# Row numbers from the one-hot table made by GpSimd instead of VectorE, with spread vectors and convolution taps in other places, in a hybrid decoder step

## The chip, the cores and the metric

The kernel runs on one core of a Trainium2 chip. The metric is the device time of one execution in microseconds, smaller is better; times are medians of several runs. The core has TensorE (PE, with its weight loads as PEld), VectorE (DVE), ScalarE (ACT), GpSimd (POOL) and the queue engine SyncE (SP). All inputs start in HBM, and 16 DMA engines carry them to the on-chip memory.

## What is computed

A two-layer decoder trunk on 256 prompt tokens and 32 sample tokens (8 sequences of 4), width 1024, all in float32. Each layer has a mixing part and an expert part:

```python
h  = rmsnorm(x) @ w_in                       # columns split among the mixers and gates
yA = gelu(u) * (tril(W_s) @ layernorm(gelu(v)) + b)          # chunks of 128, 8 groups
yB = silu(layernorm(causal_depthwise(val * sigmoid(gate))))  # 31 taps
yM = attention(q, memory)                                     # 4 heads, 256 tokens
x += (sig(gA)*(yA@w_oA) + sig(gB)*(yB@w_oB) + sig(gM)*(yM@w_oM)) @ w_out

xn = rmsnorm(x);  q = xn @ wq                # 8 heads, two halves of 64
v1, i1 = top_k(q1 @ keys1, 16);  v2, i2 = top_k(q2 @ keys2, 16)
cand   = v1[:, None] + v2[None, :];  cv, ci = top_k(cand.reshape(256), 16)
eid    = i1[ci // 16] * 128 + i2[ci % 16]    # expert row numbers, of 16384
hid    = gelu(xn . u_tab[eid]);  x += sum(softmax(cv) * hid * v_tab[eid])
```

## The kernel before

**Portions, steps and pairs.** Tokens are worked in four portions: portions 0 and 1 are the two halves of layer 0 (128 prompt tokens; 128 prompt and 32 sample tokens), 2 and 3 those of layer 1. A portion first has its mixing, which ends with scores against the keys, and then 8 or 10 expert steps. A step serves 16 tokens with 8 heads, that is 128 partitions with 16 experts each, in 8 pairs (k = 0 to 7) of two experts per partition. There are 36 steps (s) and 288 pairs (t).

**A pair.** GpSimd issues two indirect gathers (L610), each of 128 rows of 8 KB, u and v side by side. They go to one of 5 slots, so pair t + 5 is asked for when TensorE has done pair t (semaphore `v_used`). VectorE makes the two dot products of u with the token's row (`dots`, L1660; the trace shows each as a custom instruction with a short read of the sum). ScalarE makes gelu and a diagonal of weights (L663, L1024), and TensorE adds the weighted v rows (L2441).

**The order of work.** Each engine walks over the pairs. Between pairs a `stepper` advances that engine's program of the next portion's mixing as far as `reach` allows, by a table of places (`parts`, PLACE). So portion m + 1's mixing runs beside portion m's experts, in an order that is fixed for every engine. Only portion 0's mixing has no experts beside it (the first 290 us).

**Picking experts.** For step s + 1, VectorE does `pick_pairs` after the dots of pair k = 0 of step s: the sums of candidates, the top 16 of 256, and the semaphore `cmax`. After the dots of k = 1 it does `pick_experts` (L1619 to L1639). The candidate's number is split in two, a one-hot table of 32 x 16 is made, multiplied by the key numbers and summed, and 128 times the one number plus the other is written to `ids`, with the semaphore `ids`, for which the first gather of step s + 1 waits. `scale_fold` (L1672) makes the gate-weighted fold matrices, `shift` gives `cmax`. The two halves' top 16 of step s + 2 (`pick_half`) follow k = 6 and 7.

**Taps.** The causal convolution of a portion's prompt tokens is 62 taps: `conv(n)` does the next n of them. A tap is four VectorE instructions of 128 x 128 (L1131; L1129 for the first tap of a half). `beside(name, n)` and `gated(first, last, taps)` place them between the other steps of the mixing. Semaphore `conv` tells TensorE that all are done, for the sums over channels (`csum`).

**SP's queue.** SP issues the weight pieces of 1 MB in a ring of 4 (L474), each when TensorE has done with the piece four before. Some go to places of their own (`kept`, `kept_half`). In between it issues stores and other loads, each with its own wait: convolution states are stored behind the last `glu` of a portion (L532 to L534). The spread vectors (L550, L552) are four small vectors of layer 0, each repeated to 128 partitions by DMA, into parts of the expert buffers that portion 0's mixing does not use otherwise.

Of the kernel before, what the change touches and what calls it, by code (L numbers as in the profile page):

```python
# [12 lines left out]
P = 128  # L13
# [26 lines left out]
PAIRS = 8  # L40
# [200 lines left out]
def build(nc, x_in, consts_in, mem_in, cache_in, state_in, w_in, small_in, vecs_in, fing_in, ws_in, wss_in,  # L241
          keys_in, uv_in, y_out, memk_out, memv_out, convp_out, convs_out, vn_out):
    with ExitStack() as ctx:
# [193 lines left out]
        def _(sp):  # L437
# [63 lines left out]
            for m in range(PORTIONS):  # L501
# [9 lines left out]
                for n, it in enumerate(items(m)):  # L511
# [34 lines left out]
                    if m == 0 and (kind, i) == ("mg", 12):  # L546
                        sp.dma_start(x[:, 1], x_in[:, 1]).then_inc(x_landed[1], 16)
                    if m == 0 and (kind, i) == ("va", 2):
                        for to, rows in ((ln_rows[0], LN_G), (ln_rows[1], LN_B), (bs_rows, BS)):
                            sp.dma_start(to, vecs_in[rows, :].rearrange("k c -> (k c)").unsqueeze(0).to_broadcast([P, D])).then_inc(  # L550
                                spread_landed, 16)
                        sp.dma_start(ffn_row, vecs_in[FFN_G, :].rearrange("k c -> (k c)").unsqueeze(0).to_broadcast([P, D])).then_inc(row_landed, 16)  # L552
# [31 lines left out]
        def _(pool):  # L584
            def gather(t):
# [22 lines left out]
                for i in range(2):  # L608
# [4 lines left out]
                    ).then_inc(uv_landed[b], 16)  # L613

            def mixing(m):
                l, p = m // 2, m % 2
# [34 lines left out]
            for m in range(PORTIONS):  # L651
                mix = first if m == 0 else stepper(mixing(m + 1)) if m + 1 < PORTIONS else None
                for u in range(PAIRS * STEPS[m % 2]):
                    t = PAIRS * FIRST[m] + u
                    if t + SLOTS < PAIRS * NSTEP:
                        gather(t + SLOTS)
                    if mix:
                        mix(reach(m + 1, u - 1))
# [430 lines left out]
        def _(dve):  # L1089
# [29 lines left out]
            def mixing(m):  # L1119
# [164 lines left out]
                else:  # L1284
# [4 lines left out]
                    V.tensor_tensor(ys, ys, conv_b.unsqueeze(2).to_broadcast([P, KB, T_S]), ALU.add).then_inc(S["conv_s"], 1)  # L1289
                    yield from beside("q0", 1)  # L1290
                    yield from att_max(0)
                    yield from beside("q1", 2)
                    yield from att_max(1)
                    yield from beside("q2", 1)
                    att_norm(0)
# [11 lines left out]
                    if m in CACHED:  # L1307
# [8 lines left out]
                        max_sample(1)  # L1316
                    yield place["va3"]
                for t in range(1 + p):
                    r = ROWS[t]
# [146 lines left out]
                else:  # L1466
                    taps = 1 if m in CACHED else 3
                    yield from gated(0, 3, taps)
# [4 lines left out]
                    yield from spatial()  # L1473
                    yield from gated(8, 12, 3)
                    conv(2 * CONV_W)
# [51 lines left out]
            def pick_half(s, half):  # L1527

                if half == 0:
                    m = next(i for i in range(PORTIONS) if s < FIRST[i + 1])  # L1530
                    dve.wait_ge(S["score"], at("score", m, s - FIRST[m] + 1 if m else s))
# [22 lines left out]
            def pick_pairs(s):  # L1554

                sum_pairs()
                top16(cand_v, cand_i, cand, rest)
                dve.drain()
                shift(s)
# [23 lines left out]
            def pick_first():  # L1583
# [32 lines left out]
                shift(0)  # L1616

            def pick_experts(s, l):
                V.tensor_scalar(ab_u[:, 0:16], cand_i, 4, None, ALU.logical_shift_right)  # L1619
                V.tensor_scalar(ab_u[:, 16:32], cand_i, 15, None, ALU.bitwise_and)  # L1620
                dve.drain()
                V.tensor_copy(ab_f, ab_u)
                dve.drain()
                oh3 = onehot.rearrange("p (k a) -> p k a", a=16)
                V.tensor_tensor(oh3, ab_f.unsqueeze(2).to_broadcast([P, 32, 16]),  # L1625
                                iota16.unsqueeze(1).to_broadcast([P, 32, 16]), ALU.is_equal)
                dve.drain()
                for half in range(2):
                    part = oh3[:, 16 * half:16 * half + 16]
                    V.tensor_tensor(part, part, top_if[:, 16 * half:16 * half + 16].unsqueeze(1).to_broadcast([P, 16, 16]), ALU.mult)  # L1630
                dve.drain()
                V.tensor_reduce(pick_k, oh3, AX.X, ALU.add)
                dve.drain()
                V.scalar_tensor_tensor(out=eid_f, in0=pick_k[:, 0:16], scalar=float(NK), in1=pick_k[:, 16:32], op0=ALU.mult, op1=ALU.add)
                dve.drain()
                if s == NSTEP - 1:
                    for half in range(2):
                        V.tensor_scalar(ids_last[:, 2 * half:2 * half + 2], eid_f[:, 14:16], 2.0, float(2 * NEXP * l + half), ALU.mult, ALU.add)
                V.tensor_scalar(ids[:, 16 * (s % 2):16 * (s % 2) + 16], eid_f, float(NEXP * l), None, ALU.add).then_inc(S["ids"], 1)  # L1639

# [81 lines left out]

            def layer(s):
                return next(i for i in range(PORTIONS) if s < FIRST[i + 1]) // 2

            V.memset(one, 1.0).then_inc(one_set, 1)
# [9 lines left out]
            for m in range(PORTIONS):  # L1736
                mix = first if m == 0 else stepper(mixing(m + 1)) if m + 1 < PORTIONS else None
                for u in range(PAIRS * STEPS[m % 2]):
# [6 lines left out]
                    if k == 0 and s + 1 < NSTEP:  # L1745
                        pick_pairs(s + 1)
                    elif k == 1 and s + 1 < NSTEP:
                        pick_experts(s + 1, layer(s + 1))
                    elif k == 3 and s + 1 < NSTEP:
# [811 lines left out]
```

## Time and profile before

| | |
|---|---|
| median of 3 runs | 2242.09 us (2241.83 to 2243.29) |
| the profiled execution | 2242.79 us, span 2241.0 us |
| PE, DVE, ACT, POOL busy | 73%, 71%, 29%, 30% of the span |
| DMA | 895.56 MB, mean 400 GB/s |
| of it by gathers (software queue) | 604.02 MB |

A busy share is an average over stages with different limits. The profile's row of DMA over 40 slices of the span reads 9 (90% or more) in most slices, so it has to be read with the GB/s beside it, which lie at 421 or so in the full slices. DMA shares can read a little over 1. An idle time in brackets behind a row is that engine's idle time just before it, and the name is who ended it.

### The profile page before, as it was taken

How to read it: one execution, taken by the hardware profiler on the slowest of the kernel's cores; microseconds unless marked ns; L12 is line 12 of the kernel's file. 1: busy time of each engine (PE TensorE's matmuls, PEld its weight loads, DVE VectorE, ACT ScalarE, POOL GpSimd, SP SyncE). 2: the span in 40 equal slices, each digit the busy share in tenths (PEclk: the TensorE clock that was granted, in tenths of full speed). 3: DMA queues.
4: the chain of work that ended last, by engine and by line, in shares of the span. 5: the costliest groups of instructions: out<-in, count | busy, mean ns of one | idle time of the engine just before them, and what ended most of it. 6: DMA issues, size and time to landing. Idle time of an engine off the chain costs nothing.

```text
span 2241.0 us, 31369 instructions
## 1 busy us (share of the span) xinstructions
PE 1631.8 (73%) x10944; PEld 1068.0 (48%) x10944; DVE 1582.7 (71%) x4234; ACT 656.3 (29%) x1647; POOL 674.7 (30%) x596
## 2 busy tenths in 40 slices
PE   9999986889797477878788547776999854334334
PEld 8855675667585144644434315643877620000002
DVE  4454289898766667877776568977876686776775
ACT  3121243411423241423123223342223323322222
POOL 0000032232232432332223243221323354454443
PEclk9999998899897588899889777876999875555556
DMA  8699899999999999999999999999999999999998
GB/s 298 245 379 413 322 408 421 402 404 358 366 402 419 421 421 421 421 421 421 421 377 422 421 421 421 421 403 405 404 419 421 411 393 421 422 421 421 422 421 334
DMA packets 127772, 895.56 MB, mean 400 GB/s; under 512 B 16096, under 2 KB 16928, under 8 KB 20480
## 3 DMA queue, kind: packets, MB, share of 16 engines
q0 software_dynamic: 83232, 604.02, 65.4%
q1 hardware_dynamic: 44384, 289.54, 32.1%
q8 instruction: 88, 1.44, 0.3%
q14 instruction: 68, 0.56, 0.1%
HBM read 885.39 MB, written 8.11 MB: 399 GB/s over the span
## 4 chain that ended last, share of the span: by engine, by line
DMA 32%; PE 31%; DVE 21%; issue 8%; ACT 4%; DVEq 3%; POOL 2%; SPq 0%; POOLq 0%; ACTq 0%
DMA uv<-uv_in,idx_u 23%; PE bank L1785 14%; DVE uv L1660 10%; DMA ring<-w_in 7%; PE bank L2441 5%; PE bank L1791 4%; PE bank L2097 3%; DVE yB L1131 3%; DMA ring<-cache_in 2%; POOL uv L610 1%; ACT L663 1%; DVE x L1683 1%; DVEq L1126 1%; ACT diag L1024 1%; DVE pick L1625 1%
## 5 line engine op out<-in xcount | busy, mean ns | idle before, releaser
L610 POOL DMA_INDIRECT uv<-uv_in,idx_u x574 | 658.5, 1147 | 1345.5 <-PE bank L2441 642.9
L1660 DVE CUSTOM_DVE_ANT_0 uv<-uv,xrep 128x1024 f32<-128x1024 f32 x576 | 682.2, 1223 | 210.5 <-DMA uv<-uv_in,idx_u 204.7
L2441 PE MATMUL bank<-uv,diag 128*32 128x512 f32 x2176 | 393.5, 804 | 461.5 <-ACT diag L1024 457.2
L1785 PEld LDWEIGHTS bank<-xnT,ring 128*128 128x128 f32 x3168 | 433.9, 201 | 77.9 <-issue 66.4
L1785 PE MATMUL bank<-xnT,ring 128*128 128x160 f32 (+1 forms) x3168 | 456.0, 304 | 2.1 <-DMA ring<-w_in 2.0
L663 ACT ACTIVATE pick<-pick 128x2 f32<-128x2 f32 (+1 forms) x315 | 66.9, 212 | 1054.1 <-DVE pick L1660 1051.1
L2441 PEld LDWEIGHTS bank<-uv,diag 128*32 128x32 f32 x2176 | 49.8, 122 | 649.7 <-ACT diag L1024 590.7
L1131 DVE SCALAR_TENSOR_TENSOR yB<-ext_p,small,yB 128x128 f32<-128x128 f32 x960 | 275.6, 349 | 19.6
L663 ACT ACT_TABLE_LOAD x137 | 175.8, 1283 | 2.4
L1024 ACT ACTIVATE diag<-gated_fold,pick 128x32 f32<-128x32 f32 x574 | 153.1, 314 | 9.8 <-ACT pick L663 0.3
L2097 PE MATMUL bank<-ring,xnT 128*128 128x512 f32 x192 | 86.7, 605 | 0.0
L1785 PE MATMUL bank<-yMA,ring 128*128 128x160 f32 x512 | 76.9, 306 | 5.0 <-ACT yMA L663 5.0
L1785 PEld LDWEIGHTS bank<-yMA,ring 128*128 128x128 f32 x512 | 73.7, 196 | 5.2 <-ACT yMA L663 5.2
L663 ACT ACTIVATE phase<-bank 128x512 f32<-128x512 f32 (+2 forms) x44 | 23.3, 529 | 168.1 <-PE bank L1785 67.1
L1008 ACT ACTIVATE xrep<-xnf 32x1024 f32<-32x1024 f32 x64 | 67.4, 1053 | 1.4
L1791 PE MATMUL bank<-ring,ext_s 128*128 128x256 f32 x256 | 60.6, 397 | 0.0
L663 ACT ACTIVATE yMA<-bank 128x256 f32<-128x256 f32 (+2 forms) x54 | 22.2, 410 | 129.2 <-PE bank L1785 71.7
L2097 PE MATMUL bank<-ring,yMA 128*128 128x512 f32 x128 | 58.0, 605 | 1.2 <-DMA ring<-w_in 1.2
L2434 PE MATMUL bank<-uv,diag 128*32 128x256 f32 x256 | 28.6, 588 | 41.4 <-ACT diag L1024 40.8
L2097 PEld LDWEIGHTS bank<-ring,xnT 128*128 128x128 f32 x192 | 36.2, 193 | 46.1 <-issue 44.8
L663 ACT ACTIVATE sg<-bank 128x160 f32<-128x160 f32 (+1 forms) x80 | 23.6, 295 | 117.1 <-PE bank L1785 116.9
L1785 PE MATMUL bank<-ext_s,ring 128*128 128x256 f32 x256 | 57.1, 381 | 0.0
(323 smaller groups left out, 1844.4 us busy)
## 6 DMA issues: line engine op xcount, KB each, us to landing
ring<-w_in SPq DMA_DIRECT2D x211, 1024.0 KB
uv<-cache_in SPq DMA_DIRECT2D x16, 1024.0 KB, 9.7
ring<-cache_in SPq DMA_DIRECT2D x16, 1024.0 KB
uv<-uv_in,idx_u POOLq DMA_INDIRECT x578, 13.9
uv<-w_in SPq DMA_DIRECT2D x4, 1024.0 KB, 10.0
ring<-w_in SPq DMA_DIRECT2D x6, 512.0 KB, 4.9
ext_s<-state_in SPq DMA_DIRECT2D x2, 1088.0 KB, 16.7
convs_out<-ext_s SPq DMA_DIRECT2D x2, 1088.0 KB
```

Of the source, the lines that this page charges most:

```text
L610: nc.gpsimd.indirect_dma_start(out=uvbuf[2 * b + i], out_offset=None, in_=uv_in, in_offset=bass.IndirectOffsetOnAxis(ap=ids[:, c:c + 1], a ...
L663: ins = nc.scalar.activation(out, in_, func, bias=bias, scale=scale, **({} if accum is None else {"accum_out": accum}))
L1008: ins = nc.scalar.activation(xrep[gg % 2][32 * i:32 * (i + 1), :], xnf[1 if t == 2 else 0][r0:r0 + 32], ACT.Copy)
L1024: ins = nc.scalar.activation(diag[:, t % 4, i], gated_fold[:, c], ACT.Copy, scale=gel[:, 16 * (s % 2) + c:16 * (s % 2) + c + 1])
L1126: dve.drain()
L1131: ins = V.scalar_tensor_tensor(out=yB[:, c, 0:P], in0=ext_p[:, c, w:w + P], scalar=wconv[:, c, w:w + 1], in1=yB[:, c, 0:P], op0=ALU.mult, ...
L1660: ins = V.tensor_tensor_reduce(out=u, in0=u, in1=xrep[gg % 2][:, :], scale=1.0, scalar=0.0, op0=ALU.mult, op1=ALU.add, accum_out=hid[:, c: ...
L1785: ins = MM(out, w[:, k, P * b:P * (b + 1)], rhs(k), start=k == 0, stop=k == KB - 1)
L1791: ins = MM(out, lhs(k), w[k], start=k == 0, stop=k == KB - 1)
L2097: ins = MM(out[:, :], rows[:, 4 * (i % 2) + k, 0:P], w[:, k, :], start=i % 2 == 0 and k == 0, stop=i % 2 == 1 and k == 3)
L2434: ins = MM(vbank[gg % 2][32 * q:32 * (q + 1), 0:256], diag[:, t % 4, i], uvbuf[2 * b + i][:, c:c + 256], start=first and i == 0, stop=last ...
L2441: ins = MM(vbank[gg % 2][c:c + 32, :], diag[:, t % 4, i], uvbuf[2 * b + i][:, D + 512 * n:D + 512 * (n + 1)], start=first, stop=last)
```

## The change

The change has three parts. The row numbers are made by GpSimd: VectorE makes the one-hot table at the end of `pick_pairs`, before it gives `cmax`; GpSimd waits for `cmax` behind the gathers of the pair that k = 0 frees, and does the multiplication, a sum in four halving steps, the two steps of the number and the copy to `ids`. VectorE waits for `ids` before it writes the shared buffer again. The spread vectors are issued behind the load of mk 1 instead of va 2. And 16 taps of portion 1 stand elsewhere: one more at q0 and at q2 and two more at va3, one less at each of the columns 0 to 7, one more at each of the columns 8 to 11.

```diff
-                    if m == 0 and (kind, i) == ("va", 2):
+                    if m == 0 and (kind, i) == ("mk", 1):
                         for to, rows in ((ln_rows[0], LN_G), (ln_rows[1], LN_B), (bs_rows, BS)):
...
+            def pick_experts(s):
+
+                l = next(i for i in range(PORTIONS) if s < FIRST[i + 1]) // 2
+                pool.wait_ge(S["cmax"], s + 1)
+                oh3 = onehot.rearrange("p (k a) -> p k a", a=16)
+                oh4 = onehot.rearrange("p (h k a) -> p h k a", h=2, a=16)
+                G = nc.gpsimd
+                G.tensor_tensor(oh4, oh4, top_if.rearrange("p (h a) -> p h a", h=2).unsqueeze(2).to_broadcast([P, 2, 16, 16]), ALU.mult)
+                for n in (8, 4, 2):
+                    G.drain()
+                    G.tensor_tensor(oh3[:, :, 0:n], oh3[:, :, 0:n], oh3[:, :, n:2 * n], ALU.add)
+                G.drain()
+                G.tensor_tensor(pick_k.unsqueeze(2), oh3[:, :, 0:1], oh3[:, :, 1:2], ALU.add)
+                G.drain()
+                G.tensor_scalar(eid_f, pick_k[:, 0:16], float(NK), float(NEXP * l), ALU.mult, ALU.add)
+                G.drain()
+                G.tensor_tensor(eid_f, eid_f, pick_k[:, 16:32], ALU.add)
+                G.drain()
...
+                G.tensor_copy(ids[:, 16 * (s % 2):16 * (s % 2) + 16], eid_f).then_inc(S["ids"], 1)
...
                     if t + SLOTS < PAIRS * NSTEP:
                         gather(t + SLOTS)
+                    if t % PAIRS == 0 and t // PAIRS + 1 < NSTEP:
+                        pick_experts(t // PAIRS + 1)
                     if mix:
                         mix(reach(m + 1, u - 1))
...
-                    yield from beside("q0", 1)
+                    yield from beside("q0", 1 if m in CACHED else 2)
...
-                    yield from beside("q2", 1)
+                    yield from beside("q2", 1 if m in CACHED else 2)
...
                     yield place["va3"]
+                    if m == 1:
+                        conv(2)
...
-                    taps = 1 if m in CACHED else 3
+                    taps = 1 if m in CACHED else 2
...
-                    yield from gated(8, 12, 3)
+                    yield from gated(8, 12, 3 if m in CACHED else 4)
...
                 if half == 0:
+                    dve.wait_ge(S["ids"], s)
...
                 sum_pairs()
                 top16(cand_v, cand_i, cand, rest)
+                dve.drain()
+                V.tensor_scalar(ab_u[:, 0:16], cand_i, 4, None, ALU.logical_shift_right)
+                V.tensor_scalar(ab_u[:, 16:32], cand_i, 15, None, ALU.bitwise_and)
+                dve.drain()
+                V.tensor_copy(ab_f, ab_u)
+                dve.drain()
+                V.tensor_tensor(onehot.rearrange("p (k a) -> p k a", a=16), ab_f.unsqueeze(2).to_broadcast([P, 32, 16]),
+                                iota16.unsqueeze(1).to_broadcast([P, 32, 16]), ALU.is_equal)
                 dve.drain()
                 shift(s)
...
-            def pick_experts(s, l):
...
-                    elif k == 1 and s + 1 < NSTEP:
-                        pick_experts(s + 1, layer(s + 1))
```

SP's queue in portion 0, before, from the cached pieces ahead of va 2 on (names are destination and source; `uv<-vecs_in` are the spread vectors):

```order
L483 DMA uv<-cache_in 128x2048 x2
L467 DMA ring<-w_in 128x1024
L472 DMA kept_half<-w_in 128x1024
L550 DMA uv<-vecs_in 128x1024 x3
L552 DMA uv<-vecs_in 128x1024
L454 DMA kept<-w_in 128x2048
L540 DMA memv_out<-phase 128x2048
```

And in the changed kernel, where they stand now:

```order
L516 DMA ext_s<-mem_in 128x2048
L518 DMA x<-x_in 32x1024
L474 DMA ring<-w_in 128x2048 x7
L550 DMA uv<-vecs_in 128x1024 x3
L552 DMA uv<-vecs_in 128x1024
L474 DMA ring<-w_in 128x2048 x5
L483 DMA uv<-cache_in 128x2048 x2
```

The four transfers went from in front of `kept` to between the seventh and the eighth of those twelve ring pieces.

VectorE in the third step of portion 0, before, from the end of the dots of k = 1 to portion 1's normalisation statistics (BN_STATS):

```order
L1660 ISA pick 128x1
L1619 TENSOR_SCALAR idx_u<-idx_u 128x16
L1620 TENSOR_SCALAR idx_u<-idx_u 128x16
L1622 CAST pick<-idx_u 128x32
L1625 TENSOR_TENSOR pick<-pick,consts 128x512
L1630 TENSOR_TENSOR pick<-pick 128x256 x2
L1632 TENSOR_REDUCE pick<-pick 128x32
L1634 SCALAR_TENSOR_TENSOR pick<-pick 128x16
L1639 TENSOR_SCALAR idx_u<-pick 128x16
L1672 TENSOR_TENSOR gated_fold<-consts,pick 128x256
L1322 BN_STATS stat<-phase 128x6 x2
```

The same place in the changed kernel, from the end of `pick_pairs` on (L1593 makes the table, L1674 is the dots, L1157 the taps, L1350 the statistics):

```order
L1593 TENSOR_TENSOR pick<-pick,consts 128x512
L1581 TENSOR_SCALAR pick<-pick,stat 128x1
L1674 ISA uv,pick<-uv,xrep 128x1024
L1674 ISA pick 128x1
L1674 ISA uv,pick<-uv,xrep 128x1024
L1674 ISA pick 128x1
L1157 SCALAR_TENSOR_TENSOR yB<-ext_p,small,yB 128x128 x8
L1350 BN_STATS stat<-phase 128x6 x2
```

The table is made ahead of the dots of k = 1, the rest has left VectorE, two taps stand in front of the statistics, and the fold's scaling has gone behind them.

GpSimd, before, around portion 1's mixing:

```order
L640 AFFINE_SELECT phase<-phase 128x1024
L628 COPY ext_p<-ext_p 128x8x30
L610 DMA uv<-uv_in,idx_u 128x2048 x58
L640 AFFINE_SELECT phase<-phase 128x1024
L643 AFFINE_SELECT phase<-phase 32x256
```

And in the changed kernel, for the first of its 35 steps with row numbers:

```order
L610 DMA uv<-uv_in,idx_u 128x2048 x12
L622 TENSOR_TENSOR pick<-pick 128x512
L625 TENSOR_TENSOR pick<-pick 128x32x8
L625 TENSOR_TENSOR pick<-pick 128x32x4
L625 TENSOR_TENSOR pick<-pick 128x32x2
L627 TENSOR_TENSOR pick<-pick 128x32
L629 TENSOR_SCALAR pick<-pick 128x16
L631 TENSOR_TENSOR pick<-pick 128x16
L637 CAST idx_u<-pick 128x16
L610 DMA uv<-uv_in,idx_u 128x2048 x16
```

Eight operations stand between the gathers of pair 5 and those of pair 6, and so in every step: between the gathers that k = 0 and k = 1 free.

## Rows read from the trace of the kernel before

**Rows 1.** Busy time by engine, clock, DMA share, GB/s, in portion 0's mixing.

```profile
core 0: us, PE busy (x) PEld busy (x) DVE busy (x) ACT busy (x) POOL busy (x), PEclk, DMA share, GB/s
40.00:50.00 10.00, 9.98 (x58) 9.11 (x59) 7.43 (x26) 1.45 (x4) 0.00 (x0) 1.00 0.44 147
140.00:150.00 10.00, 6.72 (x36) 4.83 (x34) 3.41 (x13) 1.21 (x4) 0.00 (x0) 0.83 0.99 415
160.00:220.00 60.00, 60.00 (x328) 34.94 (x329) 26.60 (x73) 5.58 (x11) 1.48 (x2) 1.00 1.01 420
```

**Rows 2.** The same view of later stretches.

```profile
480.00:520.00 40.00, 29.73 (x183) 25.18 (x185) 37.66 (x108) 7.26 (x20) 9.71 (x10) 0.87 0.96 373
560.00:600.00 40.00, 27.27 (x179) 22.37 (x177) 31.11 (x72) 12.12 (x25) 9.01 (x9) 0.87 0.89 344
650.00:1120.00 470.00, 349.42 (x2251) 223.20 (x2249) 341.31 (x920) 140.25 (x361) 153.49 (x140) 0.83 1.01 421
1120.00:1200.00 80.00, 69.05 (x226) 30.24 (x227) 59.70 (x153) 29.49 (x60) 19.74 (x18) 0.89 0.99 391
1800.00:1810.00 10.00, 5.69 (x91) 2.00 (x89) 9.18 (x27) 3.02 (x13) 5.54 (x5) 0.99 0.88 328
1840.00:2160.00 320.00, 121.87 (x504) 12.73 (x504) 239.68 (x589) 94.63 (x247) 153.73 (x127) 0.50 1.01 421
```

**Rows 3.** TensorE in order of time: start, us, line, operation, [idle before <-releaser].

```profile
131.12 3.72 PE L1791 MATMUL bank<-ring,xnT 128*128 128x256 f32 x16
...
143.88 5.41 PE L1791 MATMUL bank<-kept,xnT 128*128 128x256 f32 x16 [3.28 <-DMA kept<-w_in]
...
159.98 7.35 PE L2097 MATMUL bank<-ring,yMA 128*128 128x512 f32 x16 [1.16 <-DMA ring<-w_in]
```

**Rows 4.** SP's queue in order of time.

```profile
127.26 1.47 SPq L550 DMA_DIRECT2D uv<-vecs_in  x3
...
129.29 0.45 SPq L454 DMA_DIRECT2D kept<-w_in  x1
```

**Rows 5.** VectorE in order of time, the third step's pick.

```profile
426.59 0.17 DVE L1619 TENSOR_SCALAR idx_u<-idx_u 128x16 uint32<-128x16 uint32 x1
...
427.94 0.76 DVE L1630 TENSOR_TENSOR pick<-pick 128x256 f32<-128x256 f32 x2
...
429.88 0.42 DVE L1672 TENSOR_TENSOR gated_fold<-consts,pick 128x256 f32<-128x256 f32 x1
```

**Rows 6.** VectorE and TensorE in order of time, portion 1's mixing.

```profile
439.04 1.43 PE L1785 MATMUL bank<-yMA,ring 128*128 128x160 f32 x4 [5.00 <-ACT yMA L663]
...
461.87 3.57 DVE L1131 SCALAR_TENSOR_TENSOR yB<-ext_p,small,yB 128x128 f32<-128x128 f32 x12
...
548.66 0.32 DVE L1352 SCALAR_TENSOR_TENSOR sg<-sg,bank 128x160 f32<-128x160 f32 x1 [0.81 <-ACT sg L663]
...
573.30 4.57 PE L2166 MATMUL bank<-yB,consts 128*128 128x160 f32 x16 [5.11 <-DVE yB L1131]
```

**Rows 7.** GpSimd and VectorE side by side at 482 us; GpSimd's copy by line.

```profile
480.40 3.92 DVE L1131 SCALAR_TENSOR_TENSOR yB<-ext_p,small,yB 128x128 f32<-128x128 f32 x8
482.09 1.11 POOL L640 TENSOR_SCALAR_AFFINE_SELECT phase<-phase 128x1024 f32<-128x1024 f32 x1
483.14 0.52 POOL L643 TENSOR_SCALAR_AFFINE_SELECT phase<-phase 32x256 f32<-32x256 f32 x1
...
L637 POOL COPY uv<-yMA 128x256 f32<-128x256 f32 x1 | 0.4, 399 | 93.6 <-ACT yMA L663 93.6
```

**Rows 8.** The tail: gathers of a pair on GpSimd, and that pair's dots.

```profile
1886.23 1.97 POOL L610 DMA_INDIRECT uv<-uv_in,idx_u  x1 [2.69 <-DVE idx_u L1639]
1888.50 0.94 POOL L610 DMA_INDIRECT uv<-uv_in,idx_u  x1 [0.31 <-issue]
...
1904.74 1.23 DVE L1660 CUSTOM_DVE_ANT_0 uv<-uv,xrep 128x1024 f32<-128x1024 f32 x1 [2.25 <-DMA uv<-uv_in,idx_u]
```

**Rows 9.** The chain of waits at 363 us; VectorE in order of time.

```profile
363.56 31.05 DMA ring<-w_in
...
406.38 0.42 DVE L1226 TENSOR_REDUCE stat<-bank 128x1 f32<-128x256 f32 x1 [7.13 <-PE bank L1917]
```

More of the change, by code:

```diff
@@ L613, in gather @@
                     ).then_inc(uv_landed[b], 16)
+            def pick_experts(s):
[15 more added lines that the diff above has]
+                G.drain()
+                if s == NSTEP - 1:
+                    for half in range(2):
+                        G.tensor_scalar(ids_last[:, 2 * half:2 * half + 2], eid_f[:, 14:16], 2.0, float(half), ALU.mult, ALU.add)
+                    G.drain()
+                G.tensor_copy(ids[:, 16 * (s % 2):16 * (s % 2) + 16], eid_f).then_inc(S["ids"], 1)
             def mixing(m):
@@ L1616, in pick_first @@
                 shift(0)
-            def pick_experts(s, l):
[L1619 to L1639, printed above, removed]
             def gates(s):
@@ L1721, in last_norm @@
                 V.scalar_tensor_tensor(out=y_last, in0=x_last, scalar=rstd_last, in1=fing_last, op0=ALU.mult, op1=ALU.mult).then_inc(y_rows, 1)
-            def layer(s):
-                return next(i for i in range(PORTIONS) if s < FIRST[i + 1]) // 2
             V.memset(one, 1.0).then_inc(one_set, 1)
```

## The prediction

> **What bounds the kernel now.** I read the stretches first [rows 1, 2]. DMA is the floor: from 650 to 1120 us it moves 421 GB/s at a busy share of 1.01, and again from 1840 to 2160 us, where the expert rows alone are fetched. In such a stretch nothing that VectorE saves or loses is seen, as long as gathers keep coming. Time can be won or lost only where DMA falls short. There are four such places. In the first 290 us no gather runs, and TensorE is full but for a hole at 140 us, where DMA is full, while it was 0.44 busy at 40 to 50 us [rows 1]. From 400 to 640 us, where portion 1's mixing runs beside portion 0's experts, DMA falls to 344 GB/s at its lowest. Two short ones follow, at 1120 to 1200 and at 1800 to 1810 us [rows 2]. Then I read who waits for whom in each.
>
> The hole at 140 us is TensorE waiting 3.28 us for the kept weights and 1.16 us for ring weights; 16 matmuls that take 3.72 us at the full clock took 5.41 us behind the hole [rows 3]. The kept weights are issued on SP's queue right behind the four spread vectors [rows 4]. From 406 to 640 us the chain of waits changes hands. VectorE begins at 406.38 behind TensorE, and from then to 434 us has no wait of note; TensorE stands 5.00 us for what follows from it at 439.04 [rows 5, 6]. From 439 to 456 TensorE leads. From 456 to 508 VectorE is full (37.66 of 40 us at 480 to 520 [rows 2]); from 508 to 548 TensorE leads; from 548 to 573.30 VectorE does, and TensorE stands 5.11 us for the convolution [rows 6]. After that TensorE and ScalarE lead to 650 us.
>
> **Part 1, the spread vectors: -5.0 us.** They are 4 transfers of 0.5 MB. At 421 GB/s that is 5.0 us of DMA taken out of the full stretch ahead of the kept weights, and 2 us of issuing [rows 4]. At their new place, behind the load of mk 1, which waits for the seventh of eight glu pieces, they run ahead of 60 us, where DMA is under half busy; q 1 stands behind them and is needed two weight pieces later. That is the cover; without it they would cost up to their 5.0 us again. What TensorE can win is 3.28 + 1.16 us of waits and 5.41 - 3.72 = 1.7 us of slow matmuls, 6.1 us; but the ring weights at 159.98 come through a DMA that stays full, and can be only 5.0 us earlier. So 5.0, at least 2 (issue time alone).
>
> **Part 2, the row numbers: what VectorE gives up.** In a step (the third, as all of them), the four instructions from L1619 to L1625 take 426.59 to 427.94 us, 1.3 us, and move to the pair before. The rest, L1630 to L1639, ends at 429.88: 1.9 us, which leaves VectorE [rows 5]. Cost if nothing else happened: -1.9 us for each step that VectorE leads.
>
> **What GpSimd takes back.** The trace has no two-input operation on GpSimd, so I bound it. A copy of 256 elements took 0.40 us, a select of 1024 1.11 us [rows 7]: 0.16 us plus 0.93 ns an element. The eight new operations are 512, 256, 128, 64, 32 and three times 16 elements. The three large ones are 1.3 us at this rate and 2.1 us if a second input doubles it; the five small ones 0.2 us each. And such an operation holds VectorE up. While GpSimd did its two selects at 482 us (1.11 and 0.52 us), eight taps that take 2.4 us elsewhere took 3.92 [rows 6, 7], 1.5 us more: the first select cost about its own length, the short one a third of it. I take 2.1 + 5 x 0.07 = 2.4 us lost per step where VectorE has two-input work all the time, the two-read end for the large ones, since these are two-input, and the short select for the small ones. Ends: 0 if a multiply or add of GpSimd does not exclude VectorE as the select did, 3.1 us if the small ones block at full length. So a step that VectorE leads changes by -1.9 + 2.4 = +0.5 us, not by -1.9. The Trainium skill (SBUF - State Buffer, "SBUF: two separate sides") says that GpSimd and a VectorE instruction with two SBUF inputs take an exclusive lock for a whole instruction, which speaks against this change; [rows 7] agree for the long select. It also prices a GpSimd two-input add of 2048 elements at 4.5 us (GPSIMD Engine Reference, "Elementwise - side-by-side cycle accounting"); by that the large three would be an estimated 2.0 us and the step about the same. No row here shows such an add.
>
> The steps that count: three in portion 1's mixing (the third, fourth and fifth), one at 1120 and one at 1805 us. In the third, GpSimd begins behind its gathers, and part of its work falls on the normalisation statistics, which read one input; 1.9 us there, so 0. The last two give +0.5 each. The other 30 lie under a full DMA.
>
> GpSimd's gathers stand behind the new work. In the tail the pair whose dots run at 1904.74 is issued from 1886.23 to 1889.4 [rows 8]. Less 5.0 us for its own 2 MB and 3 us that I allow for latency, it could be issued 7 us later without being missed. The row numbers would begin some 2 us ahead of 1886.23, behind the gathers of the pair before, so they may last some 9 us; I expect 3 to 5. Cost 0. SP does not stand behind GpSimd.
>
> **The moved 1.3 us before the stores.** SP waits for the last glu block of portion 1, then issues the stores and, from 363.56 us, loads; the piece of va that TensorE stands for lands 31 us later [rows 9]. In that step the 1.3 us now lie ahead of the glu block: +1.3 us (0 if the full DMA evens it out).
>
> **Part 3, the taps.** 12 instructions take 3.57 us with the end of the last [rows 6], so a tap (four) is 1.21 us. Two more (q0, q2) fall before 406 us, where VectorE has 7.13 us to spare [rows 9]: 0. Two more ahead of the statistics are on the path to 439.04: +2.4. Of the eight taken from columns 0 to 7, three lie where TensorE leads: 0; five lie between 456 and 508: -6.05. Four more in columns 8 to 11 give +4.84, less 0.81 us that VectorE waited at 548.66 [rows 6]: +4.0. There the scaling of the fold (0.42 us) now stands behind the taps: -0.4. Taps in all: 2.4 - 6.05 + 4.0 - 0.4 = -0.05 us.
>
> **Sum.** -5.0 (spread), +1.3 (glu block), steps 0 + 0.5 + 0.5 in portion 1, -0.05 (taps), +0.5 + 0.5 later: -1.75 us. The profiled execution took 2242.8 us (span 2241.0), so 2241.0; the median of the runs shown is 0.7 us under it: 2240.4.
>
> **Rivals.**
> VectorE isn't blocked. For it: only one place in the trace shows the blocking at length, and GpSimd may run where VectorE waits or does one-input work (max, find index). Against it: behind the pick come dots and taps, all two-input. Five steps then give -1.9 instead of up to +0.5: 0.0 - 4 x 2.4 - 1.9 = -11.5 us against the forecast, 2229; blocked by half, 2234.6. Chance 0.27.
> The spread vectors give little: at 160 to 220 us DMA is at 420 GB/s [rows 1] and could be the limit just behind TensorE. Then -2 in place of -5: 2243.4. Chance 0.11.
> TensorE takes up portion 1's additions, since VectorE's and TensorE's leads alternate and each hides some of the other's: +4.0 at 548 us halves, 2238 or a little under. Chance 0.06.
> Slower: the row numbers come too late. If each of the eight operations waits for a dot product of 1.22 us in turn, they take 3 + 8 x 1.22 = 12.8 us. From 9 us on, each further us empties the DMA queue once per step; over some 26 steps under a full DMA, 12.8 us would be +99 us, and 10 us already +26. For it: gathers already stretch from 0.94 to 1.97 us beside dots [rows 8]. Against it: in the tail VectorE has 10 us of 40 free [rows 2]. A milder form, the upper bound of blocking in all five steps and the third step too (+0.7 each, +1.2 there) with the stores' delay doubled, is 2246. Chance of over 0.2% slower: 0.14.
> The forecast itself: 0.42, its own range 2236 to 2245.
>
> **How the numbers follow.** About 0.2%, 4.5 us, can be told from no change, so faster means below 2237.6. That is the first rival (0.27), the third where it falls there (0.04) and the low end of the forecast (0.07): 0.38. Slower: 0.14 and the high edge of the second, 0.16. Same: 0.46. The range reaches down to most of the first rival, 2230, and up to the mild slow case, 2247.
>
> **What the profile after would show.** No wait for the kept weights near 140 us, and the first gather 5 us earlier. GpSimd's eight operations, some 3 us in sum, and taps or dots beside them of 1.9 us in place of 1.22. From the first dots to the convolution's end at 573 us about the same distance (+1 to +5 us from 456 being lost and won again), DMA at 420 again from 650 us. I am wrong if the dots beside GpSimd's operations keep 1.22 us, if the stretch from 400 to 640 us shrinks by 5 us or more, or if DMA falls under 415 GB/s in the tail.

## The result: 220 us slower

| kernel | median | runs | to the kernel before, 95% interval |
|---|---|---|---|
| before | 2242.69 us | 4 (2241.83 to 2247.23) | |
| changed | 2462.47 us | 4 (2461.13 to 2463.80) | 1.0977 (1.0963 to 1.0991) |

The forecast was 2240.4 us, its range 2230 to 2247. One of the four executions of a kernel further down, the one with sixteen fills, took 4397 us beside three of 2313 to 2325 us, and its median and ratio are those of the three. The page of the changed kernel, its span, VectorE's and DMA's rows over 40 slices, and the chain of waits:

```profile
span 2462.1 us, 31650 instructions
PE 1651.1 (67%) x10944; PEld 1077.4 (44%) x10944; DVE 1581.7 (64%) x4057; ACT 656.2 (27%) x1647; POOL 796.2 (32%) x878
...
DMA  8799999998988899899999889899998888788878
GB/s 311 281 395 364 371 367 408 376 380 345 392 364 352 352 386 379 361 410 377 383 405 381 344 341 396 329 420 399 379 408 337 354 354 350 295 358 350 352 293 350
DMA packets 127775, 895.58 MB, mean 364 GB/s; under 512 B 16096, under 2 KB 16928, under 8 KB 20480
...
issue 27%; PE 25%; DMA 22%; DVE 11%; POOL 6%; POOLq 5%; ACT 2%; DVEq 2%; SPq 0%
```

The bytes are the same, the rate has gone from 400 to 364 GB/s, and of the slices that read 421 before none is left (the best reads 420). VectorE is as busy as before (1582.7 us then). "issue" with 27% is time in which an engine stood for nothing that the profile names. The stretches, in the columns of [rows 1]:

```profile
650.00:1120.00 470.00, 317.44 (x2033) 202.28 (x2032) 301.60 (x767) 133.22 (x340) 175.64 (x193) 0.80 0.91 373
1840.00:2160.00 320.00, 143.51 (x1078) 61.69 (x1077) 191.77 (x453) 83.90 (x226) 133.09 (x144) 0.62 0.83 341
```

Against [rows 2], 421 GB/s became 373 beside mixing (the first stretch) and 341 in the tail (the second): the floor itself has holes. What the change brought to GpSimd's queue comes once per step, so I looked there. GpSimd and VectorE in order of time, in one step of the tail (L610 the gathers, L622 the multiplication, L625 the three larger additions, L637 the copy to `ids`, L1674 the dots):

```profile
2225.94 1.07 POOL L610 DMA_INDIRECT uv<-uv_in,idx_u  x1 [0.30 <-issue]
2227.02 1.45 POOL L622 TENSOR_TENSOR pick<-pick 128x512 f32<-128x512 f32 x1
...
2244.03 1.23 DVE L1674 CUSTOM_DVE_ANT_0 uv<-uv,xrep 128x1024 f32<-128x1024 f32 x1 [3.50 <-DMA uv<-uv_in,idx_u]
2244.55 3.11 POOL L625 TENSOR_TENSOR pick<-pick 128x256 f32<-128x256 f32 x3 [16.08 <-issue]
2245.18 1.73 DVE L1674 CUSTOM_DVE_ANT_0 uv<-uv,xrep 128x1024 f32<-128x1024 f32 x1
...
2248.90 0.20 POOL L637 CAST idx_u<-pick 128x16 uint32<-128x16 f32 x1
2249.65 0.99 POOL L610 DMA_INDIRECT uv<-uv_in,idx_u  x1 [0.55 <-POOL idx_u L637]
```

The multiplication starts at once behind the gathers, and then GpSimd stands for 16.08 us. Between the two lies only the first `G.drain()` (L624). It ends at 2244.5, half a us after the dots of the last pair issued (2244.03) found their rows landed. That half a us comes back: in 20 of the 35 steps VectorE stood waiting for that same pair, and in every one of the 20 the drain ended 0.51 or 0.52 us after these dots began. In the other 15 VectorE was not waiting, so its rows don't show the landing. The same stretch by DMA, in the columns of [rows 1]:

```profile
2238.00:2242.00 4.00, 0.96 (x8) 0.20 (x8) 2.38 (x4) 0.73 (x3) 0.00 (x0) 0.50 0.91 377
2242.00:2243.00 1.00, 1.00 (x8) 0.00 (x0) 0.00 (x0) 0.00 (x0) 0.00 (x0) 0.50 0.04 16
...
2245.00:2250.00 5.00, 1.93 (x8) 0.20 (x8) 2.51 (x5) 0.74 (x3) 3.58 (x8) 0.50 0.00 0
2250.00:2252.00 2.00, 0.00 (x0) 0.00 (x0) 0.00 (x0) 0.00 (x0) 1.57 (x2) 0.50 0.46 66
```

DMA has nothing to move from 2242 to about 2251 us, 9 us in this step. The order is what matters: first DMA runs dry, then the drain ends, then come 5.1 us of the other seven operations, then the next gather. All steps together, by line:

```profile
L625 POOL TENSOR_TENSOR pick<-pick x105: 291/1021/2304, 324.5 to 2397.6; 128x256 f32<-128x256 f32 x35, 128x128 f32<-128x128 f32 x35, 128x64 f32<-128x64 f32 x35
its engine sat idle before it (us, times) until:
  issue: 667.5, 37
```

667.5 us in 35 steps is 19 us a step; the wait is 9.5 us in the first step, where less was under way, and up to 30.9. The two longest, of 30.7 and 30.9 us, stand beside mixing, where the weights share DMA. One such wait ended at 888.96 us; the queues' shares from 884 to 888 us, then from 888 to 891 us (q0 is GpSimd's gathers, q1 is SP's transfers; the columns are packets, MB and share of the 16 engines):

```profile
q0 software_dynamic: 156, 1.09, 65.5%
...
q1 hardware_dynamic: 125, 0.89, 71.5%
```

The gathers had ended, transfers of SP were under way, and GpSimd went on. These were young, though: SP had issued them at 886.08 us, after the drain had begun at 863.4, and by bytes no older transfer of SP outlasted a drain in any of the 35 steps of this trace. So the working theory, W: a drain on GpSimd waits for every gather that GpSimd itself issued before it, and for nothing of SP's; the last part is still open here, and a later kernel settles it.

### The profile page after: what moved, and what is told of

Same layout as the page of the kernel before. It is cut to its first block, busy times and chain, and to the rows that moved or that the text cites. A ratio compares the mean times of both kernels' runs of the same rounds, so it can differ in the third digit from the quotient of the medians.

```text
span 2462.1 us, 31650 instructions
## 1 busy us (share of the span) xinstructions
PE 1651.1 (67%) x10944; PEld 1077.4 (44%) x10944; DVE 1581.7 (64%) x4057; ACT 656.2 (27%) x1647; POOL 796.2 (32%) x878
## 4 chain that ended last, share of the span: by engine, by line
issue 27%; PE 25%; DMA 22%; DVE 11%; POOL 6%; POOLq 5%; ACT 2%; DVEq 2%; SPq 0%
DMA uv<-uv_in,idx_u 19%; PE bank L1794 10%; DVE uv L1674 5%; POOL uv L610 5%; PE bank L2450 5%; PE bank L1800 3%; POOLq L624 3%; DVE yB L1157 2%; PE bank L2106 2%; DMA ring<-w_in 2%; DMA ring<-cache_in 1%; POOL pick L622 1%; ACT diag L1050 1%; DVEq L1152 1%; DVEq L1561 1%
## 5 line engine op out<-in xcount | busy, mean ns | idle before, releaser
L1674 DVE CUSTOM_DVE_ANT_0 uv<-uv,xrep 128x1024 f32<-128x1024 f32 x576 | 703.6, 1259 | 464.6 <-DMA uv<-uv_in,idx_u 449.8
L2450 PE MATMUL bank<-uv,diag 128*32 128x512 f32 x2176 | 404.5, 825 | 659.4 <-ACT diag L1050 644.4
L610 POOL DMA_INDIRECT uv<-uv_in,idx_u x574 | 595.4, 1037 | 748.7 <-PE bank L2450 352.8
L625 POOL TENSOR_TENSOR pick<-pick 128x256 f32<-128x256 f32 (+2 forms) x105 | 90.2, 859 | 677.1 <-issue 667.5
L1157 DVE SCALAR_TENSOR_TENSOR yB<-ext_p,small,yB 128x128 f32<-128x128 f32 x960 | 288.0, 361 | 19.9 <-issue 0.4
L2106 PEld LDWEIGHTS bank<-ring,xnT 128*128 128x128 f32 x192 | 36.3, 194 | 47.0 <-issue 45.1
L1800 PEld LDWEIGHTS bank<-ring,ext_s 128*128 128x128 f32 x256 | 50.5, 200 | 12.5 <-issue 5.4
## 6 DMA issues: line engine op xcount, KB each, us to landing
uv<-uv_in,idx_u POOLq DMA_INDIRECT x578, 15.6
convs_out<-ext_s SPq DMA_DIRECT2D x2, 1088.0 KB, 16.2
```

The source lines that it names most:

```text
L610: nc.gpsimd.indirect_dma_start(out=uvbuf[2 * b + i], out_offset=None, in_=uv_in, in_offset=bass.IndirectOffsetOnAxis(ap=ids[:, c:c + 1], a ...
L625: G.tensor_tensor(oh3[:, :, 0:n], oh3[:, :, 0:n], oh3[:, :, n:2 * n], ALU.add)
L1157: ins = V.scalar_tensor_tensor(out=yB[:, c, 0:P], in0=ext_p[:, c, w:w + P], scalar=wconv[:, c, w:w + 1], in1=yB[:, c, 0:P], op0=ALU.mult, ...
L1674: ins = V.tensor_tensor_reduce(out=u, in0=u, in1=xrep[gg % 2][:, :], scale=1.0, scalar=0.0, op0=ALU.mult, op1=ALU.add, accum_out=hid[:, c: ...
L1800: ins = MM(out, lhs(k), w[k], start=k == 0, stop=k == KB - 1)
L2106: ins = MM(out[:, :], rows[:, 4 * (i % 2) + k, 0:P], w[:, k, :], start=i % 2 == 0 and k == 0, stop=i % 2 == 1 and k == 3)
```

## The experiments

**Drains replaced by semaphores.** Everything else stays as in the changed kernel.

```diff
+                def link(ins):
+                    nonlocal n_done
+                    n_done += 1
+                    ins.then_inc(pick_done, 1)
+                    pool.wait_ge(pick_done, n_done)
...
-                    G.drain()
-                    G.tensor_tensor(oh3[:, :, 0:n], oh3[:, :, 0:n], oh3[:, :, n:2 * n], ALU.add)
+                    link(G.tensor_tensor(oh3[:, :, 0:n], oh3[:, :, 0:n], oh3[:, :, n:2 * n], ALU.add))
```

> The changed kernel with each drain between GpSimd's operations replaced by a semaphore that the operation raises and the next one waits for. Theory W (the drain waits until every gather that GpSimd issued before it has landed): the 13 to 20 us between the multiply and the first addition vanish, the eight operations take some 6 us, DMA is back at 415 to 421 GB/s in the tail, and the time is near the forecast, 2236 to 2247 us. Rival C (the wait belongs to GpSimd's computing beside gathers: any operation that follows another one there stands until the gathers have landed): the wait stays and the time is 2455 to 2465 us. Rival L (the operations are too slow because VectorE holds the memory lock): the wait is spread over the eight operations, 2300 to 2460 us.

Measured: 2237.24 us, ratio 0.9970 (0.9961 to 0.9979). The whole 220 us hang on the drains, and rivals C and L fall. GpSimd in order of time in the tail, the step in which the row numbers take longest (L631 multiplication, L633 to L636 the sums, L641 the copy), and the tail's stretch:

```profile
1959.47 1.27 POOL L631 TENSOR_TENSOR pick<-pick 128x512 f32<-128x512 f32 x1
1960.81 5.82 POOL L633 TENSOR_TENSOR pick<-pick 128x256 f32<-128x256 f32 x3
1966.72 1.10 POOL L634 TENSOR_TENSOR pick<-pick 128x32 f32<-128x32 f32 x1
...
1970.19 0.20 POOL L641 CAST idx_u<-pick 128x16 uint32<-128x16 f32 x1
...
1840.00:2160.00 320.00, 122.31 (x516) 13.29 (x512) 239.97 (x554) 94.83 (x247) 196.86 (x189) 0.51 1.01 421
```

No gap is left behind the multiplication, and DMA is at 421 GB/s again. From the multiplication's start to the copy's end it takes 5.95 us as a mean of the 35 steps, 4.2 to 10.9.

**A lone drain in the kernel before.** The other way round: nothing of the change but one drain.

```diff
                     if t + SLOTS < PAIRS * NSTEP:
                         gather(t + SLOTS)
+                    if t % PAIRS == 0 and t // PAIRS + 1 < NSTEP:
+                        nc.gpsimd.drain()
```

> The kernel before, with one lone drain on GpSimd per step, behind the gathers that k = 0 frees, and nothing else. Theory W: the next gather is issued only when all ten ahead of it have landed; the changed kernel's DMA was empty for some 7.5 us per step, of which some 5.5 were the operations behind the wait, so 2 us per step remain, and 35 steps give about +70 us, 2290 to 2335 us. Rival C: a drain with no computing before it has nothing to wait for, 2241 to 2244 us.

Measured: 2371.10 us, ratio 1.0565 (1.0549 to 1.0582), +128 us. Theory W holds and rival C falls, but the time lies above W's range: my price, +70 us, was about half of it. GpSimd in two steps of the tail:

```profile
2078.49 1.97 POOL L610 DMA_INDIRECT uv<-uv_in,idx_u  x1 [16.67 <-PE bank L2443]
...
2124.48 1.98 POOL L610 DMA_INDIRECT uv<-uv_in,idx_u  x1 [16.95 <-PE bank L2443]
...
1840.00:2160.00 320.00, 125.66 (x732) 33.63 (x736) 211.21 (x523) 90.39 (x246) 125.17 (x112) 0.57 0.89 363
```

The view puts the 16.67 us down to TensorE, on whose semaphore this gather waits too; but TensorE had done the pair whose slot it takes by 2065.0 us (the matmuls from 2063.02), and the only new thing ahead of the gather is the drain. DMA ran dry at about 2076.2 us, the gather behind the drain starts 2.3 us later, at 2078.49, and data flow again from 2081.0 us, 2.5 us behind its start: 4.8 us empty. In the first two us after that, at 172 and then 287 GB/s, some 0.9 us more are lost. I had counted 2. Forgotten were the time by which the drain's end lags behind the data and the restart of a queue from empty. A step takes 46.0 us here; in the kernel before it took 40.6 (L1632, the sum for the row numbers, starts at 1844.66 us and seven steps later at 2129.19). These 5.4 us are the tail's; over all 35 steps 128 us are 3.7 us a step, so a step beside mixing loses less.

**One drain put back, at the end.**

```diff
                 link(G.tensor_tensor(eid_f, eid_f, pick_k[:, 16:32], ALU.add))
+                G.drain()
```

> The kernel with semaphores between GpSimd's operations (2237 us), with one drain put back: behind the last addition, ahead of the copy to ids. Theory W: the seven operations now run while the gathers land, and only the copy and the next gather stand behind the wait, so DMA is empty per step as long as with the lone drain of the kernel before (5.5 us in the tail), and the time is that kernel's 2371 less the 5 us of the spread vectors: 2355 to 2375 us. The difference from the changed kernel's 2462 is then what the operations behind its first drain cost. Rival (each of the changed kernel's drains has a share of the loss, and one in seven brings a seventh of it): 2265 to 2275 us.

Measured: 2368.47 us, ratio 1.0559 (1.0543 to 1.0576), within W's range; the rival of equal shares falls.

```profile
2144.81 1.45 POOL L631 TENSOR_TENSOR pick<-pick 128x512 f32<-128x512 f32 x1
...
2150.44 0.22 POOL L636 TENSOR_TENSOR pick<-pick 128x16 f32<-128x16 f32 x1
2161.37 0.78 POOL L642 CAST idx_u<-pick 128x16 uint32<-128x16 f32 x1 [10.71 <-issue]
```

The operations hide in the wait (5.8 us of it), which ends as late as it would without them: 16.6 us behind the multiplication's start, where the lone drain ended 16.7 us behind its gathers. So the first drain behind a gather pays and its place among the operations decides what stands behind it: 128 us for the wait, and 2462.5 - 2368.5 = 94 us more in the changed kernel for what follows its first drain.

The second step of this kernel also settles what W says of SP. SP's issues ahead of the drain, the copy behind it, and SP's queue from 363 to 380.31 us and from 380 to 381 us:

```profile
363.93 0.66 SPq L535 DMA_DIRECT2D convs_out<-ext_s  x1
364.63 5.45 SPq L475 DMA_DIRECT2D ring<-w_in  x2
...
380.31 0.21 POOL L642 CAST idx_u<-pick 128x16 uint32<-128x16 f32 x1 [14.02 <-issue]
...
q1 hardware_dynamic: 1147, 1.05, 25.1%
...
q1 hardware_dynamic: 29, 0.23, 100.1%
```

The drain began at 366.3 us. The store `convs_out` alone is 1.11 MB (1088 KB), and weight pieces of 1.05 MB each follow it; by the drain's end SP's queue had moved 1.05 MB since 363 us and was still full. The gathers had moved their last bytes by about 378 us. So transfers that SP issued before a drain don't hold it either.

**How late may the row numbers be?** Eight or sixteen fills of the used table stand ahead of the copy to `ids`, in the kernel with semaphores; they are idle work.

```diff
+                for _ in range(8):
+                    link(G.memset(onehot, 0.0))
```

> The kernel with semaphores between GpSimd's operations, with eight fills of 128x512 in a chain added ahead of the copy to ids; at 1.81 us for 2048 elements they take an estimated 4 to 5 us, so that the row numbers last some 10.5 us instead of the 5.95 us measured. By the prediction's limit of 9 us and its 26 us per us beyond it: +39 us, 2276 us. By the changed kernel's trace, where the ten gathers issued ahead kept DMA busy for some 15 us behind the multiply's start and the first new bytes came 3 us after the copy: nothing is lost up to 12 us, 2235 to 2241 us.

Measured: 2259.37 us, ratio 1.0060 (1.0045 to 1.0076); the row numbers last 10.6 us as a mean.

> The same with sixteen fills, some 9 to 10 us, so that the row numbers last some 15 us. By the prediction's limit: 6 x 26 = +156 us, 2393 us. By the reading of the changed kernel's trace (12 us free): 3 us too late in 26 to 35 steps, +80 to +105 us, 2315 to 2342 us.

Measured: 2313.99 us, ratio 1.0336 (1.0311 to 1.0361); 15.2 us as a mean. GpSimd in a step of the tail of the second (L638 the fills), its DMA around that step, and the stretch from 650 us of the first:

```profile
2145.69 1.44 POOL L631 TENSOR_TENSOR pick<-pick 128x512 f32<-128x512 f32 x1
...
2160.90 0.20 POOL L643 CAST idx_u<-pick 128x16 uint32<-128x16 f32 x1
...
2155.00:2165.00 10.00, 3.98 (x20) 0.52 (x24) 6.28 (x13) 3.41 (x11) 8.36 (x14) 0.50 0.66 250
...
650.00:1120.00 470.00, 346.45 (x2215) 220.83 (x2213) 339.86 (x876) 139.25 (x357) 232.20 (x280) 0.82 1.01 417
```

With 10.6 us the full stretch stays full (417 GB/s), and the kernel loses 22 us, where my new reading said 0 and the prediction's limit +42 at the same 10.6 us. Both were off: by the starts of the multiplications, some 5 of the 22 us are lost in the first step and the rest in some six steps of 3 to 5 us each (other steps give a little back), the one where the row numbers last 15.6 us among them. With 15.2 us every tail step loses. In all it is +77 us by the medians and +82 by the ratios, at the low end of what the 12 us limit gave (both against the kernel with semaphores). A tail step takes 40.5 us with semaphores alone, 41.0 where the row numbers last 11.5 us and 45.1 where they last 16.2. So the limit is near 11 us in the tail, not 9, and it is one of each step, not of the mean; the first 25 steps, beside mixing, lose only 26 us together in the kernel with sixteen fills.

**The row numbers alone**, with semaphores, in the kernel before.

> The kernel before with the row numbers made by GpSimd, with semaphores in place of drains, and neither the spread vectors nor the taps moved. By the prediction +1.3 for the 1.3 us ahead of the glu block and +0.5 for each of four steps: 2245 to 2246.5 us. By the run with semaphores, which stood within 0.5 us of the spread vectors alone: 2241 to 2244 us, since what VectorE gave up (1.8 us a step) and what it lost beside GpSimd (1.7 us a step by its rows) are equal.

Measured: 2245.12 us, ratio 1.0012 (1.0002 to 1.0021), within the range by the prediction's terms. SP's store of portion 0's states, of the kernel before and then of this one, where the first gathers start at 288.45 and 287.72 us:

```profile
362.18 0.64 SPq L532 DMA_DIRECT2D convp_out<-ext_p  x1
```

```profile
363.92 0.64 SPq L533 DMA_DIRECT2D convp_out<-ext_p  x1
```

Counted from the first gather the store comes 73.7 us later before and 76.2 us later here. The predicted delay of 1.3 us is 2.5 in this pair of traces. Over all traces the store comes 72.8 to 74.4 us behind the first gather in the five kernels that make the row numbers on VectorE without a drain, and 76.2 to 78.0 us behind it in the four that make them on GpSimd with semaphores and no fills, 3.5 us between the means. Ahead of the last glu block stand four multiplications of the sample tokens' convolution (L1170, L1140 in the kernel before) with two inputs each, and GpSimd's multiplication and additions (358.94 to 362.1 us) fall right on them:

```profile
358.95 3.38 DVE L1170 TENSOR_TENSOR merged<-ext_s,small 128x248 f32<-128x248 f32 x4
```

In the kernel before they take 1.40 us.

**The spread vectors and the taps alone.**

```diff
-                    if m == 0 and (kind, i) == ("va", 2):
+                    if m == 0 and (kind, i) == ("mk", 1):
```

> The kernel before with only the spread vectors moved. By the changed kernel's trace, where the first gather came 5.4 us earlier: 2236.5 to 2238.5 us. Rival (the earlier start is lost to a DMA that is full anyway from 290 us on, since it moves the same bytes later): it can't be lost where DMA is the floor, but some of it can fall on portion 1's mixing, then 2239 to 2242 us.

Measured: 2237.70 us, ratio 0.9973 (0.9961 to 0.9984). In the changed kernel the kept weights' matmuls have no wait and run at full speed; its SP's queue, TensorE and first gather:

```profile
36.85 1.66 SPq L550 DMA_DIRECT2D uv<-vecs_in  x3
...
140.68 3.62 PE L1800 MATMUL bank<-kept,xnT 128*128 128x256 f32 x16
...
149.52 3.70 PE L2106 MATMUL bank<-ring,xnT 128*128 128x512 f32 x8 [0.59 <-DMA ring<-w_in]
...
283.08 1.12 POOL L610 DMA_INDIRECT uv<-uv_in,idx_u  x1 [85.19 <-DVE idx_u L1618]
```

The granted clock at 140 to 150 us is 1.00, where it was 0.83 [rows 1]. The time lies within the expected range.

> The kernel before with only the 16 taps moved. By the prediction -0.05 us, 2241 to 2243 us. Rival (the two taps ahead of the statistics lie on the path and nothing is given back later, since the columns 0 to 7 wait for TensorE): +2.4 to +4, 2244.5 to 2246.5 us.

Measured: 2243.03 us, ratio 0.9999 (0.9990 to 1.0008), as the prediction had it; the rival of +2.4 to +4 us falls.

**Do the parts add up?** Four kernels on one chip: the spread vectors with one other part each, the spread vectors alone, and all three with semaphores.

> The spread vectors moved and the row numbers made by GpSimd with semaphores; the taps stay where they were. If the three parts add up: -5.2 and +2.2 (the row numbers alone took 2245.1), 2240 us. If what GpSimd's row numbers cost is made good by the taps' new places, this is the one that shows it: 2240 us here and 2237 with the taps moved. Rival (the +2.2 of the row numbers alone are lost once the mixing starts 5 us earlier, and the taps do nothing): 2237 us here too.

> The spread vectors and the taps moved, the row numbers left on VectorE. The taps alone did nothing (2243.0 against 2243.0), so 2236.5 to 2239 us, as the spread vectors alone. If the taps' places only suit a VectorE that doesn't make the row numbers: 1 to 3 us slower than the spread vectors alone.

> The spread vectors alone once more, on the chip that runs the two combinations, since 2 us are to be told apart: 2236.5 to 2239 us.

> All three parts with semaphores once more, for the same reason. If the parts add up, 2240 us, 2 to 3 us above the spread vectors alone; if the taps make the row numbers' cost good, 2236 to 2238 us.

| parts | median | ratio |
|---|---|---|
| spread vectors | 2237.73 us | 0.9972 (0.9961 to 0.9983) |
| spread vectors, taps | 2236.87 us | 0.9969 (0.9957 to 0.9981) |
| spread vectors, row numbers | 2239.56 us | 0.9980 (0.9968 to 0.9991) |
| all three | 2241.45 us | 0.9984 (0.9975 to 0.9993) |

The kernel before took 2244.64 us here. The medians say that the row numbers cost 2 to 5 us and the taps nothing, but the intervals overlap, and the same kernel with all three parts stood level with the spread vectors alone in the first run (0.9970 against 0.9973). The row numbers on GpSimd bring no gain in any of the four comparisons; whether they cost 0 or 4 us on top of the others stays open. That the taps' places make good what they cost isn't borne out. The best kernel here is the kernel before with the spread vectors moved, with or without the taps: 0.3% faster than before, 9% faster than the changed one.

## Why the prediction was wrong

**The step that failed** is "GpSimd's gathers stand behind the new work … so they may last some 9 us; I expect 3 to 5. Cost 0." I costed the eight operations and took the seven drains between them at nothing, as on VectorE, where `dve.drain()` stands between operations everywhere. On GpSimd the first drain behind the gathers waits for them. From the multiplication's start to the copy's end it took 25.2 us as a mean of the 35 steps, 19.05 of them in the gap behind the multiplication. The trace of before holds no drain on GpSimd with gathers under way, so it could not show this; but it was an instruction without a row, and such a one has to be bounded from both sides. The upper bound was there to read: all gathers under way, ten of 1 MB, which at 421 GB/s are 25 us, and more where the weights share DMA. Of the prediction's own signs of being wrong, DMA under 415 GB/s in the tail is the one that came: 341.

**The slower rival** had the right place and the wrong mechanism. It let each operation wait for a dot product. That exists: 10.9 us in the longest step with semaphores. It is rare, and the mean is 5.95 us, under every limit. Its own price, 26 us per us beyond 9, set in 2 us too early and was too high: 15.2 us cost 77 to 82 us, not 161, and counted from 11 us the same price would still give 109.

**The duration of the operations**: 3 to 5 us expected, 5.95 measured. The multiplication and the first two additions, put at 2.1 us (2.0 by its second estimate), took 1.37 + 1.06 + 0.91 = 3.3 us by their means in the kernel with semaphores, where VectorE stands in their way at times.

**What VectorE gains and loses**: -1.9 and +2.4 us a step. Measured, of the kernel before by line: dots, taps, fold, and what was moved away;

```profile
L1660 DVE CUSTOM_DVE_ANT_0 uv<-uv,xrep 128x1024 f32<-128x1024 f32 x576 | 682.2, 1223 | 210.5 <-DMA uv<-uv_in,idx_u 204.7 <-issue 4.5
L1131 DVE SCALAR_TENSOR_TENSOR yB<-ext_p,small,yB 128x128 f32<-128x128 f32 x960 | 275.6, 349 | 19.6
...
L1672 DVE TENSOR_TENSOR gated_fold<-consts,pick 128x256 f32<-128x256 f32 x72 | 30.4, 423 | 0.3 <-issue 0.2
L1630 DVE TENSOR_TENSOR pick<-pick 128x256 f32<-128x256 f32 x70 | 26.6, 422 | 2.6
...
L1632 DVE TENSOR_REDUCE pick<-pick 128x32 f32<-128x512 f32 x35 | 24.0, 686 | 2.6
```

and of the kernel with semaphores:

```profile
L1678 DVE CUSTOM_DVE_ANT_0 uv<-uv,xrep 128x1024 f32<-128x1024 f32 x576 | 703.8, 1260 | 216.1 <-DMA uv<-uv_in,idx_u 200.7 <-issue 14.1
L1161 DVE SCALAR_TENSOR_TENSOR yB<-ext_p,small,yB 128x128 f32<-128x128 f32 x960 | 289.1, 363 | 19.9 <-issue 0.4
...
L1690 DVE TENSOR_TENSOR gated_fold<-consts,pick 128x256 f32<-128x256 f32 x72 | 44.8, 623 | 0.1
```

The two instructions shown and two small ones (6.2 and 6.8 us) are 63.6 us less, 1.8 a step. Dots, taps and fold are 49.5 us longer, four smaller groups another 10: 1.7 a step. So the gain is 0, and VectorE's busy time is 1582.7 us before and 1585.6 with semaphores. That VectorE would be held up was right (a dot product beside an addition took 1.73 us, at 2245.18 above, for 1.22). 1.7 is a mean over all steps, though, and the 2.4 were meant for a step in which VectorE has two-input work all the time, so it can't be called 0.7 too much; that the four multiplications above lost 2.0 us rather speaks for it. One reading behind the 2.4 was off: of the 1.5 us that the eight taps lost, 1.1 are the long select's, and the 0.4 left are three quarters of the short one's 0.52 us, not a third. The Trainium skill (SBUF - State Buffer, "SBUF: two separate sides") says that a GpSimd operation that reads SBUF and a VectorE instruction with two SBUF inputs exclude each other, and these rows agree that such VectorE instructions get longer (the fold's 423 ns became 623).

**The row numbers in all**: the prediction's terms give +3.3 us, the run gave +2.7 by its ratio (0.4 to 4.7). That the total fits is partly luck: the delay of the stores, predicted at 1.3 us, was 2.5 in one pair of traces and 3.5 by the means, because the prediction left out that GpSimd's operations fall on two-input work there. What made up for it isn't shown.

**The spread vectors**: -5.0 predicted, the runs give -6.1 and -6.3 by ratio, within the interval. The mechanism was right: no wait at 140 us, first gather 5.4 us earlier, ring weights still a little late (0.59 us).

**The taps**: -0.05 predicted, -0.2 (-2.2 to +1.8) measured. That the sum comes out is shown, that its terms of 2 to 6 us each do is not.

Without the drains the forecast of -1.75 us would have stood against -6.7 and -3.6 us in the two runs of the kernel with semaphores, 2 to 5 us too high. The failure is one term of 220 us.

## What to carry to other kernels

On an engine that issues its own gathers, order dependent operations by a semaphore that each raises and the next waits for, never by a drain: here that was worth 225 us of 2462, for the same eight operations. The Trainium skill (GPSIMD Engine Reference, "Instruction dispatch") asks for a wait on the producer's completion semaphore where a GpSimd operation reads partitions that another of its cores wrote in the operation before, because the cores don't wait for each other. The operations here stay within their partitions, and no run leaves both drain and semaphore out, so whether they need either isn't shown; what a drain in the semaphore's place costs behind gathers is. When a change puts a new instruction on a queue, bound it by all that this queue has under way, also where the instruction seems to do nothing. And where DMA is the floor, ask when it runs dry: work of 6 us between two batches of gathers cost 0 to 5 us in all, 15 us another 77 to 82.

## What the runs showed of the hardware that I had not expected

- A drain on GpSimd ended only when GpSimd's own gathers had landed, 16 us later in the tail and up to 30.9 us later beside the weights' transfers, while SP's transfers under way did not hold it, neither those issued after it nor those issued before it (1.05 MB of at least 1.24 MB moved at its end). The six drains behind it cost some 0.1 to 0.2 us each (0.16 us idle between the instructions of L627 and L629).
- Restarting from an empty queue costs on its own: the gather behind the lone drain started 2.3 us after DMA ran dry, and data flowed 2.5 us after that, 4.8 us in which next to nothing moved.
- An operation that waits for a semaphore raised by the one before it started some 0.08 us after its end.
- Four VectorE multiplications of 128 x 248 beside GpSimd's multiplication and additions took 3.38 us, and 1.40 us without.
- Not tried: whether a drain on SP or ScalarE waits in the same way for transfers issued there, and whether GpSimd's drain waits for plain transfers as for gathers.
